# Feed-forward with interleaved gate and up tiles and Strassen products for three of eight K pairs

## The reference

```python
D_FF = -(-8 * D_MODEL // (3 * 256)) * 256        # 5632
...
        ffn = (jax.nn.silu(x @ w_gate[l]) * (x @ w_up[l])) @ w_down[l]
        x = layer_norm(DEEPNORM_ALPHA * x + ffn, ln_g[l, 1], ln_b[l, 1])
```

## Time and profile before

| | |
|---|---|
| runs | 1892.26, 1892.47, 1892.53 us |
| profiled execution, span from the first to the last instruction | 1889.9 us |
| median of the runs less this span | 2.6 us |
| PE matmul busy | 1876.0 us, 9647 matmuls |
| DVE busy | 1322.6 us |
| ACT busy | 919.6 us |
| DMA | 389.69 MB, mean 206 GB/s |

### The profile page before, as it was taken

One profiled execution on the slowest core, in us unless ns is written; L12 is line 12 of the kernel. 1 busy time (PEld: TensorE's weight loads), 2 busy tenths in 40 slices (PEclk: granted clock), 3 DMA queues, 4 the chain that ended last, 5 costly groups with the idle time before them and its releaser, 6 DMA issues.

```text
span 1889.9 us, 29981 instructions
## 1 busy us (share of the span) xinstructions
PE 1876.0 (99%) x9647; PEld 1548.7 (82%) x9647; DVE 1322.6 (70%) x1859; ACT 919.6 (49%) x1234; POOL 184.7 (10%) x448
## 2 busy tenths in 40 slices
PE   9999999999999999999999999999999999999997
PEld 7888888878888888888888887888888888888886
DVE  7878888888676767675677657577775466654656
ACT  5656565664455555556444447444443444443442
POOL 0202020020023233333000000000000000000000
PEclk9999999999999999999999999999999999999999
DMA  7667666575567776776665775566666666665565
GB/s 276 220 202 223 204 214 225 188 242 166 189 198 240 219 245 214 241 222 209 203 193 195 233 237 169 199 189 195 193 196 194 191 192 197 191 196 192 190 192 175
DMA packets 121041, 389.69 MB, mean 206 GB/s; under 512 B 14512, under 2 KB 27632, under 8 KB 120816
## 3 DMA queue, kind: packets, MB, share of 16 engines
q1 hardware_dynamic: 97904, 351.65, 58.2%
q10 hardware_dynamic: 19200, 28.34, 4.9%
q0 software_dynamic: 3840, 8.39, 1.6%
HBM read 368.91 MB, written 19.42 MB: 205 GB/s over the span
## 4 chain that ended last, share of the span: by engine, by line
PE 97%; DVE 1%; DMA 0%; issue 0%; ACT 0%; SPq 0%; DVEq 0%; ACTq 0%
PE pg L496 92%; PE B L496 5%; DVE gates L1474 1%; DMA raw<-in_weights 0%; PE B L596 0%; ACT whi L870 0%; PE B L816 0%; DVE wlo L1466 0%; DVE act_b L1466 0%; PE B L744 0%; DVE lnst L2170 0%; DVE sm L1474 0%; DVE act_a L1466 0%; DVE lnst L2175 0%; ACT L1390 0%
## 5 line engine op out<-in xcount | busy, mean ns | idle before, releaser
L1466 DVE TENSOR_TENSOR wlo<-raw,whi 128x1024 fp32r<-128x1024 f32 (+1 forms) x640 | 778.6, 1219 | 472.8 <-ACT whi L870 454.2
L870 ACT ACTIVATE whi<-raw 128x1024 fp32r<-128x1024 f32 (+1 forms) x640 | 674.3, 1057 | 751.8 <-PE pg L496 706.2
L496 PE MATMUL pg<-whi,act_x 128*128 128x512 f32 x2960 | 936.2, 393 | 1.0 <-ACT whi L870 1.0
L496 PEld LDWEIGHTS pg<-whi,act_x 128*128 128x128 f32 x2960 | 555.6, 188 | 120.2 <-issue 3.7
L496 PE MATMUL pg<-wlo,act_x 128*128 128x512 f32 x1480 | 574.7, 390 | 0.0
L496 PE MATMUL pg<-whi,act_a 128*128 128x512 f32 x1632 | 504.7, 389 | 0.1
L496 PEld LDWEIGHTS pg<-whi,act_a 128*128 128x128 f32 x1632 | 306.3, 188 | 64.2 <-DVE act_a L1466 0.8
L496 PEld LDWEIGHTS pg<-wlo,act_x 128*128 128x128 f32 x1480 | 278.1, 188 | 54.9
L496 PE MATMUL pg<-wlo,act_a 128*128 128x512 f32 x816 | 317.5, 389 | 0.0
L496 PEld LDWEIGHTS pg<-wlo,act_a 128*128 128x128 f32 x816 | 153.2, 188 | 31.7
L496 PE MATMUL pg<-whi,act_b 128*128 128x512 f32 x512 | 158.4, 389 | 0.0
(11 more groups left out here) (264 smaller groups left out, 1067.8 us busy)
## 6 DMA issues: line engine op xcount, KB each, us to landing
raw<-in_weights SPq DMA_DIRECT2D x646, 512.0 KB, 4.3
turn_c<-hraw ACTq DMA_DIRECT2D x8, 512.0 KB, 3.3
qT<-turn_c ACTq DMA_DIRECT2D x32, 128.0 KB, 4.5
turn_q<-hraw ACTq DMA_DIRECT2D x6, 512.0 KB, 4.5
gates<-turn_q ACTq DMA_DIRECT2D x24, 128.0 KB, 4.6
turn_p<-gates POOLq DMA_DIRECT2D x12, 192.0 KB, 3.4
gates<-turn_p POOLq DMA_DIRECT2D x48, 48.0 KB, 4.0
decm<-sums_out ACTq DMA_DIRECT2D x4, 512.0 KB, 3.9
```

Source lines behind the costliest of these rows:

```text
L496: return nc.tensor.matmul(o, l, r, start=start, stop=stop)
L870: return nc.scalar.activation(o, i, ACT.Copy, scale=scale)
L1466: return V.tensor_tensor(o, a, b, op)
```

## The change

In groups 1 to 10 the tiles of gate and up now alternate: tile s of a group is gate for even s and up for odd s, both of K pair s // 2. Three of the eight K pairs (`SPOS` = 2, 4, 6, which are tiles 4 and 5, 8 and 9, 12 and 13) are "mixed": the product of the 2 x 2 blocks of x (token half by K chunk) and the 2 x 2 blocks of weights (K chunk by gate or up) is made from seven block products in place of eight. For that DVE makes sums of weight blocks (`v13`, `v24`), ACT and DVE their high and low parts (`h13`, `h24`, `l13`, `l24`), and once, in group 0, the sums of x (`xs`). Four of the products (in the banks called `other`) are shared by the results; after tile 13 ACT copies one bank (`q1`) and DVE forms the sums from them (`shared_out`), adds them to the gate banks after tile 14 (`gate_out`) and to the up banks after tile 15 (`up_out`), ACT takes silu, and DVE multiplies (`product`, at tile 3 of the next group). Two sets of four banks (`pg` and `B`) are used in turns as `own` and `other`. The hidden block is turned by a write to DRAM and four reads from it in another order, and one transpose of 128x1024 on DVE (`turn_h`). The loops of the walk are written out on every engine.

```diff
-GAIN = (11, 13)
+GAIN = (4, 8)
+SPOS = (2, 4, 6)
+NS = len(SPOS)
+H_AT, H_AWAY, H_BACK, H_TURN, H_HI, H_LO = 3, 5, 8, 11, 12, 13
...
+            def mixed_tile(f, n, s):
...
+                if s % 2 == 0:
+                    product(other[0], act_a[:, 0, k, t0], act_a[:, 1, k, t0], whi[:, r, 0], wlo[:, r, 0], first, last)
+                    product(own[0][0], act_a[:, 0, k + 1, t0], act_a[:, 1, k + 1, t0], whi[:, r, 1], wlo[:, r, 1], False, False)
+                    product(other[3], xs[:, i, 2, 0], xs[:, i, 2, 1], v["h13"][:, 0], v["l13"][:, 0], first, last)
+                    end = product(other[2], xs[:, i, 1, 0], xs[:, i, 1, 1], v["h13"][:, 1], v["l13"][:, 1], first, last)
+                else:
+                    product(own[1][0], xs[:, i, 3, 0], xs[:, i, 3, 1], whi[:, r, 1], wlo[:, r, 1], False, False)
+                    product(other[1], xs[:, i, 0, 0], xs[:, i, 0, 1], v["h24"][:, 0], v["l24"][:, 0], first, last)
+                    end = product(own[0][1], act_a[:, 0, k + 1, t1], act_a[:, 1, k + 1, t1], v["h24"][:, 1], v["l24"][:, 1],
...
+            def own_free(f):
+
+                if f in (5, 9):
+                    pe.wait_ge(gate_free, f - 1)
+                    pe.wait_ge(up_free, f - 1)
+                elif f > 1:
+                    pe.wait_ge(shared_free, f - 1)
...
+            def mixed_item(f, n, s):
+
+                m, v, i = n + s, mixed(f), nth(f, s)
+                r = m % RING
+                if s % 2 == 0:
+                    for e in range(2):
+                        dve.wait_ge(raw_full[r + e], 16 * (m // RING + 1))
+                    tt(v["v13"], raw[:, r:r + 2, 0], raw[:, r + 1, 0:2], ALU.add).then_inc(v_sum, 1)
+                    dve.wait_ge(s_hi, 2 * i + 1)
+                    dve.wait_ge(tile_used, m - AHEAD)
+                    tt(wlo[:, r], raw[:, r], whi[:, r], ALU.subtract)
+                    dve.wait_ge(v_sum, 3 * i + 1)
+                    tt(v["v24"][:, 0], v["v13"][:, 0], raw[:, r + 1, 1], ALU.add).then_inc(v_sum, 1)
+                    dve.wait_ge(v_sum, 3 * i + 2)
+                    tt(v["v24"][:, 1], v["v24"][:, 0], raw[:, r, 1], ALU.add).then_inc(v_sum, 1)
+                    dve.wait_ge(hi_done, m + 1)
+                    dve.wait_ge(tile_used, sums_used(m, s))
+                    tt(v["l13"], v["v13"], v["h13"], ALU.subtract).then_inc(lo_done, 1)
+                else:
+                    dve.wait_ge(s_hi, 2 * i + 2)
+                    dve.wait_ge(tile_used, m - AHEAD)
+                    tt(wlo[:, r, 1], raw[:, r, 1], whi[:, r, 1], ALU.subtract)
+                    dve.wait_ge(hi_done, m + 1)
+                    tt(v["l24"], v["v24"], v["h24"], ALU.subtract).then_inc(lo_done, 1)
+
+            def shared_out(f):
+
+                v, other = mixed(f), [b[:, :] for b in banks(f)[1]]
+                dve.wait_ge(q1_done, f)
+                lnc(tt(v["w"][:, 0], v["q1"], other[1], ALU.add))
+                lnc(tt(v["u3"], v["w"][:, 0], other[2], ALU.add))
+                tt(v["w"][:, 0], other[3], v["w"][:, 0], ALU.subtract)
+                tt(v["w"][:, 1], other[3], v["u3"], ALU.subtract).then_inc(shared_free, 1)
...
+            def turn_h(f, s):
+
+                if f and s == 0:
+                    up_out(f)
+                if f and s == H_AT:
+                    product(f)
+                if s == H_TURN:
+                    dve.wait_ge(q_full, 64 * (HEADS_TURNED + f + 1))
...
+                if s == H_LO:
...
+                for s in range(0 if f else TPG + 1, 2 * TPG):
+                    if f and is_mixed(s + AHEAD):
+                        mixed_item(f, n, s + AHEAD)
+                    else:
+                        split(n, s)
+                    if f not in (0, 5, 9):
+                        turn_h(f - 1, s)
...
+                    if f and s == S_END:
+                        shared_out(f)
+                    if f and s == 2 * TPG - 1:
+                        gate_out(f)
```

More of the change, by code:

```diff
@@ L838, in _, with product @@
                             turn_x1(0, o - 4)
-            def up(n, g, cnt, place, cq=None):
-                pair_of_groups(n, g, (act_a, act_a), isinstance(n, int) and n == N_FFN)
-            def down(piece, n, g, tiles, buf, cnt, place):
-                pe.wait_ge(N["dve_mT"], 1 + cnt - 1)
+            def product(bank, xh, xl, wh, wl, start, stop):
+                mm(bank[:, :], xh, wh, start, False)
+                mm(bank[:, :], xh, wl, False, False)
+                return mm(bank[:, :], xl, wh, False, stop)
@@ new lines, in plain_tile @@
+            def plain_tile(m, x, k0, own, first, last):
+                r = m % RING
+                pe.wait_ge(hi_done, m + 1)
+                pe.wait_ge(lo_done, m + 1)
+                for k in range(TK):
+                    for t in range(TOK):
+                        a = slice(t * P, (t + 1) * P)
+                        end = product(own[t], x[:, 0, k0 + k, a], x[:, 1, k0 + k, a], whi[:, r, k, :], wlo[:, r, k, :],
+                                      first and k == 0, last and k == TK - 1)
+                end.then_inc(tile_used, 1)
@@ new lines, in mixed_tile @@
+            def mixed_tile(f, n, s):
+                own, other = banks(f)
+                v, i, k, m = mixed(f), SPOS.index(s // 2), s // 2 * TK, n + s
+                r, first, last = m % RING, i == 0, i == NS - 1
+                t0, t1 = slice(0, P), slice(P, SEQ)
+                pe.wait_ge(hi_done, m + 1)
+                pe.wait_ge(lo_done, m + 1)
+                if s % 2 == 0:
[7 more added lines that the diff above has]
+                    end = product(own[0][1], act_a[:, 0, k + 1, t1], act_a[:, 1, k + 1, t1], v["h24"][:, 1], v["l24"][:, 1],
+                                  False, False)
+                end.then_inc(tile_used, 1)
@@ new lines, in up_out, with by_head @@
+            def up_out(f):
+                v, own = mixed(f), banks(f)[0]
+                dve.wait_ge(tile_used, up_at(f) + 2 * TPG)
+                dve.wait_ge(shared_free, f)
+                for t in range(TOK):
+                    last = tt(v["w"][:, t], v["w"][:, t], own[1][t][:, :], ALU.add)
+                last.then_inc(up_free, 1)
+            by_channel = flat(hraw[:, :, :]).rearrange("p (b h t i) -> p t h b i", b=4, h=HB, t=TOK)
+            def by_head(ap):
+                return ap.rearrange("p (h b i) -> p h b i", h=HB, b=4)
@@ new lines, in product, with turn_h @@
+            def product(f):
+                dve.wait_ge(silu_done, f)
+                dve.wait_ge(up_free, f)
+                w = mixed(f)["w"]
+                if f == FG - 1:
+                    tt(hraw[:, :, :], w, vda[:, :, :], ALU.mult).then_inc(N["dve_m"], 1)
+                    return
+                for t in range(TOK):
+                    last = tt(by_channel[:, t], by_head(w[:, t]), by_head(vda[:, t]), ALU.mult)
+                last.then_inc(N["dve_m"], 1)
+            def turn_h(f, s):
+                if f and s == 0:
[4 more added lines that the diff above has]
+                    dve.wait_ge(q_full, 64 * (HEADS_TURNED + f + 1))
+                    dve.wait_ge(N["act_mT"], 1 + 2 * (NB + f))
+                    V.transpose(turned.rearrange("p h (t a x) -> p a (h t) x", t=TOK, x=SB), landed(hraw)).then_inc(N["dve_turn"], 1)
+                if s == H_LO:
+                    dve.wait_ge(N["act_mT"], 1 + 2 * (NB + f) + 2)
+                    tt(lo(*hidden(f), 4), turned, hi(*hidden(f), 4), ALU.subtract).then_inc(N["dve_mT"], 1)
```

377 lines of the change are left out of this document (261 added, 116 removed).

## The result

The kernel after takes 1920.3 us (median of 4 runs, 1917.8 to 1922.7) against 1892.4 beside it on the same chip: ratio 1.0148, 95% interval [1.0136, 1.016], 28 us slower. It was forecast at 1910.

What follows compares the result with a forecast made beforehand. PE was taken to bound the kernel, with DVE going from spare to level. Waits of 38.2 less 20.4 saved give +17.8 on the 1889.9 span, 1907.7, and 1910 us as the runs' median; range 1884 to 1936.

Steps and rivals of the forecast that it cites:

- (d): Tile 0 to 4: DVE idles behind the silu on ACT; PE waits 0.7 us in seven groups, 4.9 in all.
- (a): Tile 4 to 8: tile 9's weights, asked for late, hold DVE; PE waits 0.7 us, 1.1 with the gain, 6.1 in all.
- (c): Tile 12 to the next group: DVE waits for ACT, then makes shared sums; PE waits 2.0 us eight times, 16.0.
- (b): Tile 8 to 12: late weights, beside the product's reads from DRAM; PE waits 1.6 us in seven groups, 11.2.
- the gain: Norm's gain operations on DVE in groups 1 to 4: 2.6 us more, 42.0 of DVE work against PE's 41.5.
- The gain on PE: Feed-forward: 30 mixed pairs take 21 matmuls for 24, at 0.227 us each, so 20.4 us less on PE.
- The sum: Feed-forward: waits of 38.2 us in all, less 20.4 saved on PE, net +17.8, a span of 1907.7.
- Hidden: Rival: DVE's 39.3 us fit into PE's 41.5 per group, so waits nearly vanish: 1874 us, chance 0.19.
- Full length of each DVE operation: Rival: DVE operations follow only after their whole duration, 3.6 us more a group, 1935 us; chance 0.09.
- The clock falls: Rival: PE's clock halves for one tile after each of the eight waits (c), 22 us more, 1932; chance 0.06.

Runs made afterwards that it cites:

- experiment 2: Kernel after, with the silu later on ACT, behind the rounding of the next group's tile 3: 1913.8 us, ratio 1.0115.
- experiment 3: Kernel after, with the turned block's high part on ACT and low part on DVE one tile later: 1924.4 us, ratio 1.0171.
- experiment 4: Kernel after, without the product's write to DRAM and four reads back (hidden values in wrong order): 1908.0 us, ratio 1.0079.
- experiment 5: Kernel after, with a mixed pair's ring slots given back after their last reader, odd tile's low part made earlier: 1895.55 us, ratio 1.0018.
- experiment 10: As experiment 9, with the norm's gain and shift moved from groups 1 to 4 to the first down projection: 1876.9 us, ratio 0.9918.
- experiment 9: Kernel after with the changes of experiment 2 and experiment 5 together, reads left in place: 1880.0 us, ratio 0.9931.
- experiment 7: Kernel after, block read back and turned later, PE waiting for it only at the down projection tile using it: 1919.4 us, ratio 1.0141.
- experiment 11: Kernel after, with only the norm's gain and shift moved out of groups 1 to 4: 1921.2 us, ratio 1.0148.
- experiment 1: Kernel after with two mixed pairs (2 and 6) instead of three: 1888.95 us, ratio 0.9979.
- experiment 6: Kernel after with two mixed pairs and the later silu, the changes of experiment 1 and experiment 2: 1883.0 us, ratio 0.9948.
- experiment 8: Kernel after, three mixed pairs, with the changes of experiment 2, experiment 5 and experiment 7 together: 1889.4 us, ratio 0.9983.

## Why the prediction held, and where it was off

**The direction and the four places** were right: PE waits before tiles 4, 8, 12 and behind the shared sums, in groups 2 to 4, 6 to 8 and 10. Group 3 takes 46.96; groups 5 and 9 ran without a wait, as forecast. Each place moved by its own edit: (d) and (a) in experiment 2, (c) in 3, (b) in 4 and 5; in 10 all four are gone.

**(d) and (c)** are right in mechanism and in size: forecast 11.6 and 12.2 us from tile to tile, measured 11.65 and 12.21 to 12.27 (table above). Taken by idle times, 0.48 and 1.65, they would look smaller than the 0.7 and 2.0 forecast; the difference is what a wait costs beside its idle time, and the forecast, a lap less PE's pace, had it in.

**(a)** is right in size, 5.7 for 6.1, but two causes give the same 11.28 us. Without the gain DVE waits for the load, as worked out; with it, DVE comes straight from the gain operations and the load is there already (landed at 1316.10). First group 7, then group 3:

```profile
1586.09 1.23 DVE L1664 TENSOR_TENSOR alt_x<-raw 128x1024 f32<-128x1024 f32 x1 [1.33 <-DMA raw<-in_weights]
```

```profile
1316.50 1.22 DVE L1664 TENSOR_TENSOR alt_b<-raw 128x1024 f32<-128x1024 f32 x1
```

That the two come out alike is chance: the load took 4.6 us and not 4.3. It is why experiment 5, which lets loads be asked for early, took (a) away in groups 6 to 8 and 10 and left it in 2 to 4.

**(b)** is the term that was mis-sized: 11.2 forecast, 17.0 measured. I let the loads beside the reads land after 6.1 at most, from rows of the attention part; here they took up to 7.9. And group 1, which I had let off, paid the second most (2.75 of idle time). Experiment 4 shows the cause: without the reads (b) is 0.85 at most.

**The gain on PE** was also mis-sized: 20.4 forecast, 17.7 measured. The 21 matmuls of a mixed pair take 4.85 us and not 4.76, in every kernel here with such pairs and without any wait; 30 pairs make 2.7. PE in the last mixed pair of group 3 in experiment 10:

```profile
1320.39 1.56 PE L575 MATMUL pg<-act_b,xs 128*128 128x512 f32 x6
1321.79 0.40 PE L575 MATMUL B<-whi,xs 128*128 128x512 f32 x1
```

Six matmuls with the sums of x (`xs`) as stationary operand take 1321.79 - 1320.39 = 1.40 us, 0.233 each instead of 0.227, and 12 of the pair's 21 are such. Why that operand is slower stays open. Most groups of experiment 10 take 41.9 us and not 41.75, mainly because of their first tile, which starts as the shared sums end.

**The sum.** Waits forecast 38.2, measured 43.4 in the same terms: 5.2 more. With 2.7 less gain, 1.15 ahead of group 1 and 0.6 in small pieces this is the 9.7 us between the forecast span of 1907.7 and 1917.4. The 1.15 may be chance: in the profiles of the kernels with three mixed pairs group 1 began between 1202.8 and 1204.5 us, with the same work ahead of it, and in the kernel before at 1203.3.

**Rivals.** Hidden: refuted for this order, and true for another; experiment 10 is that case, at 1876.9 for its 1874. Whether 39.3 fits in 41.5 does not decide; that the load for a mixed pair may be asked for before the pair is done gives 25 of the 28 us, and the later silu gives the rest (experiment 9). Full length of each DVE operation: refuted, DVE's rows still follow each other after 1.14 us (1333.65 to 1334.78 to 1335.92). By full durations a group would take DVE 39.3 + 3.6 = 42.9 us, and in experiment 10 PE starts a group every 41.9. The sentence of the Trainium skill that the prediction took this rival from (VectorE: DVE Perf Modes, The DRAIN you can't avoid) is not the whole of it: the same section says that a next operation that is not held starts earlier. These rows agree with that, if they count as not held, which no run here tests. The clock falls: it happened, twice and not eight times, behind waits of 3.80 and 2.05, and not behind 2.75 or any of those of 1.7 at (c); and it cost nothing, because PE had to wait for DVE in that step in any case. My argument against it, that the clock held for 4 us of idle time at the end, did not carry over. The warning of the Trainium skill (TensorE: Matmul & The Clock Gate, HAM oscillation) was the better guide, though not every wait that comes again brought the clock down: in experiments 2, 3, 7 and 11 it was at half three to five times and in 4 once, each time in or close behind a wait of 1.8 us or more (the longest distance is 1.5 us), and where there was no such wait (experiments 1, 5, 6, 8, 9 and 10) it stayed full up to the last matmul.

## What to carry to other kernels

When vector and scalar work is added beside a full TensorE, the sum of their work does not tell whether they keep up. First follow one ring slot round its lap (last reader, load, landing, next reader) and one engine's order past each point where another waits. Give a slot back at its last reader, not at the end of the whole item: here that alone was worth 25 us with the same work. Compare times from tile to tile rather than idle times, and ask of a slow stretch whether the engine would have waited in it anyway. And before giving up an arithmetic saving that came out slower, take the waits away: the same arithmetic went from 28 us slower than before to 15.6 us faster.

## What the runs showed of the hardware

- A wait of PE delays it by more than its idle time, 0.28 us at tile 8 of group 3 (11.28 us, less 0.71 of idle time and 10.29 of work): 0.16 of it is the overlap of two matmuls' rows (0.39 long, 0.227 apart), the rest the slower first matmuls.
- Loads on SP's queue beside four reads of 128 KB on ACT's queue landed after 4.5 to 7.9 us in the kernel after where they were issued within 5 us behind the first read (up to 8.3 in experiment 3), for a median of 4.3 before, and SP's issue took up to 1.02 us for 0.33.
- In or close behind single waits of 1.80 to 3.97 us the granted clock was at half, mostly for 3.4 us, but not behind all of that length (1.80 and 2.75 in the kernel after, 2.38 and 2.61 in experiment 2, 3.04 in experiment 11): the length of the wait alone does not tell.
- A stretch at half clock cost nothing where PE was held by DVE anyway: step (c) took 12.21 and 12.26 us with 3.4 us of it, 12.21 to 12.27 without. With 6.8 us, in group 6 of experiment 2, the step took 13.21.
- Matmuls with the sums of x as stationary operand came every 0.233 us, those of plain tiles every 0.227.
